# Split products of a two-block decoder: the moving columns and their results walked from the last column to the first

## The reference, cut to what matters

```python
q = (hf @ w_query).reshape(T, PEER_HEADS, 2, D_KEY // 2)
s1 = jnp.einsum("thk,hnk->thn", q[:, :, 0], sub_keys1)
s2 = jnp.einsum("thk,hnk->thn", q[:, :, 1], sub_keys2)
...                                       # top 16 of 16384 experts for each token and head
u = expert_down[ib]                       # (128 tokens, 8 heads, 16, 1024)
act = jax.nn.gelu(jnp.einsum("td,thkd->thk", hb, u), approximate=False)
v = expert_up[ib]
return jnp.einsum("thk,thkd->td", gb * act, v)
```

## Time and profile before

| | |
|---|---|
| time, median of 3 runs | 2018.89 us (2018.7 to 2019.29) |
| profiled execution: span from first to last instruction | 2015.2 us |
| PE busy | 1988.4 us, 99% of the span |
| DVE, ACT busy | 1512.0 us (75%), 1025.4 us (51%) |
| TensorE clock granted, mean | 0.996 |
| DMA | 219 GB/s in the mean |

### The profile page before, as it was taken

One profiled execution on the slowest core, in us unless ns is written; L12 is line 12 of the kernel. 1 busy time (PEld: TensorE's weight loads), 2 busy tenths in 40 slices (PEclk: granted clock), 3 DMA queues, 4 the chain that ended last, 5 costly groups with the idle time before them and its releaser, 6 DMA issues.

```text
span 2015.2 us, 38041 instructions
## 1 busy us (share of the span) xinstructions
PE 1988.4 (99%) x14231; PEld 1842.9 (91%) x14231; DVE 1512.0 (75%) x2628; ACT 1025.4 (51%) x1394; POOL 0.2 (0%) x4
## 2 busy tenths in 40 slices
PE   9999999999999999999999999999999999999998
PEld 8888999999999888888899999999999998888886
DVE  6777779988885666666679665888888866666666
ACT  6741454455555444444546553544555554444444
POOL 0000000000000000000000000000000000000000
PEclk8999999999999999999999999999999999999999
DMA  8555767776566777777655655777766677777776
GB/s 302 177 200 190 280 202 243 237 246 200 186 187 217 238 243 238 243 240 242 208 170 168 189 165 179 226 237 229 235 196 186 187 226 238 244 238 242 239 245 189
DMA packets 136462, 440.85 MB, mean 219 GB/s; under 512 B 15136, under 2 KB 15392, under 8 KB 133920
## 3 DMA queue, kind: packets, MB, share of 16 engines
q1 hardware_dynamic: 118496, 406.84, 64.5%
q10 hardware_dynamic: 17856, 32.51, 4.4%
HBM read 403.64 MB, written 35.65 MB: 218 GB/s over the span
## 4 chain that ended last, share of the span: by engine, by line
PE 91%; DVE 5%; DMA 2%; ACT 1%; issue 1%; SPq 0%; DVEq 0%; ACTq 0%
PE ps L581 27%; PE ps L582 27%; PE ps L583 27%; PE ps L913 3%; DVE ring_lo L394 2%; PE ps L618 1%; DMA ring<-in_wq 1%; PE ps L631 1%; PE ps L761 1%; PE ps L889 1%; ACT ring_hi L388 1%; DMA arena<-in_w_ada 0%; DMA ring<-in_down 0%; DVE arena L1979 0%; DVE arena L1544 0%
## 5 line engine op out<-in xcount | busy, mean ns | idle before, releaser
L394 DVE TENSOR_TENSOR ring_lo<-ring,ring_hi 128x1024 fp32r<-128x1024 f32 x632 | 772.6, 1223 | 289.1 <-ACT ring_hi L388 285.3
L388 ACT ACTIVATE ring_hi<-ring 128x1024 fp32r<-128x1024 f32 x632 | 667.9, 1057 | 601.4 <-PE ps L583 496.1
L581 PE MATMUL ps<-h_hi,ring_lo 128*128 128x256 f32 x2816 | 801.6, 285 | 11.0 <-DVE ring_lo L394 8.6
L582 PE MATMUL ps<-h_lo,ring_hi 128*128 128x256 f32 x2816 | 789.0, 280 | 0.0
L583 PE MATMUL ps<-h_hi,ring_hi 128*128 128x256 f32 x2816 | 788.9, 280 | 0.0
L581 PEld LDWEIGHTS ps<-h_hi,ring_lo 128*128 128x128 f32 x2816 | 535.5, 190 | 15.0 <-issue 7.7
L582 PEld LDWEIGHTS ps<-h_lo,ring_hi 128*128 128x128 f32 x2816 | 532.8, 189 | 0.4 <-issue 0.2
L583 PEld LDWEIGHTS ps<-h_hi,ring_hi 128*128 128x128 f32 x2816 | 530.6, 188 | 0.0
L583 PE MATMUL ps<-ring_hi,w_hi 128*128 128x512 f32 x1024 | 399.0, 390 | 0.0
L581 PE MATMUL ps<-ring_hi,w_lo 128*128 128x512 f32 x1024 | 399.0, 390 | 0.0
L582 PE MATMUL ps<-ring_lo,w_hi 128*128 128x512 f32 x1024 | 399.0, 390 | 0.0
(11 more groups left out here) (300 smaller groups left out, 1331.4 us busy)
## 6 DMA issues: line engine op xcount, KB each, us to landing
ring<-in_down SPq DMA_DIRECT2D x256, 512.0 KB, 4.3
ring<-in_up SPq DMA_DIRECT2D x256, 512.0 KB, 4.0
ring<-in_w_in SPq DMA_DIRECT2D x72, 512.0 KB, 3.6
kept_z<-wf ACTq DMA_DIRECT2D x124, 256.0 KB, 3.2
xT<-kept_z SPq DMA_DIRECT2D x124, 256.0 KB, 4.2
arena<-in_w_ada SPq DMA_DIRECT2D x16, 1024.0 KB, 8.9
ring<-in_wq SPq DMA_DIRECT2D x32, 512.0 KB, 4.2
arena<-in_w_ada SPq DMA_DIRECT2D x16, 512.0 KB, 8.2
```

The costliest lines, as they stand in the source:

```text
L388: nc.scalar.activation(ring_hi[:, part_slot(m), :], ring[:, slot(m), :], ACT.Copy).then_inc(S("high"), 1)
L394: ns.tensor_tensor(ring_lo[:, part_slot(n), :], ring[:, slot(n), :], ring_hi[:, part_slot(n), :].bitcast(fp32), ALU.subtract)\
L581: mm(psum, s_lo, m_hi, start=start, stop=False)
L582: mm(psum, s_hi, m_lo, start=False, stop=False)
```

## The change

`product` turns three views round along their last axis before it issues its three matmuls: the PSUM destination and both parts of the moving operand.

```diff
             def product(psum, stat, move, start, stop):
 
                 (s_hi, s_lo), (m_hi, m_lo) = stat, move
+                psum, m_hi, m_lo = psum[:, ::-1], m_hi[:, ::-1], m_lo[:, ::-1]
                 mm(psum, s_lo, m_hi, start=start, stop=False)
                 mm(psum, s_hi, m_lo, start=False, stop=False)
                 return mm(psum, s_hi, m_hi, start=False, stop=stop)
```

## The result

The changed kernel takes **2045.64 us** (median of 4 runs, 2044.11 to 2046.88). The kernel before took 2018.80 us in the median of four runs (2006.13 to 2019.29); the ratio is 1.0165, with a 95% interval of 1.0135 to 1.0195. So the change costs between 1.4 and 2.0%, about 27 us. Before's own runs scatter: one of the four lies 13 us under the other three, and 13 more, taken later with the experiments, have a median of 2009.52 us. All runs of the changed kernel lie above all of them.

What follows compares the result with a forecast made beforehand. The prediction took PE's product matmuls, times the distance between their starts, to bound the kernel. A span of 2015.2 us, plus 0 for the change and 3.7 us around it, gave 2018.9 us; the range was 1987 to 2090 us.

Steps and rivals of the forecast that it cites:

- Rival B: Every product matmul: walking backwards, each crossing between memory stretches costs twice, 68 us more, about 2087 us; chance 0.06.
- Rival D: 256-column products: the 113.1 and 117.8 ns regimes shift; 1987 to 1996 us (chance 0.09) or 2029 to 2039 us (0.06).
- What bounds the kernel: On PE: 12,096 product matmuls times the distance between their starts, about 1.74 ms; DVE, ACT and DMAs lie beside it.
- The place: Product matmuls at full clock: a surcharge along the columns, 6.5 and 13.6 ns, on which a turned direction acts.
- Read of the moving columns: Product matmuls' moving operand, step -1 for +1: same elements and neighbours, so 0 us.
- Write of the sums: Product matmuls' PSUM write, step -1: all three matmuls of a product are turned alike, so 0 us.
- Rival A: Every product matmul: a backwards walk gets one column per half-clock cycle, 1484 us more, about 3503 us; chance 0.15.
- Rival C: Product matmuls: the surcharge vanishes, together 53 us faster, about 1966 us; chance 0.05.
- The weight load: 256-column matmuls: the unturned weight load bounds them at 108 ns, hiding the change if only 512-column steps move.

## Why the prediction was right and wrong

The time lies in the range, near its middle, but the forecast, 2018.9 us and no change, did not happen. By the sign that the prediction set itself, a distance that moves by more than a third of a nanosecond, it was wrong: by 4.7 ns at 300 us and by 6.5 ns at 700 us. That the range holds the time is partly luck. It was drawn around rivals B and D, and what came is D's places together with half of B's price on 512 columns, a case that the list does not have.

- *What bounds the kernel*: right. The loss is product matmuls times the distance of their starts, 27 of 29.9 us by the sum above; nothing beside PE moved. One check in it was loose: 1.74 ms is 86% of the span, and the chain's share of the three lines is 81%.
- *The place*: right. "at full clock something along the columns (the read of the moving operand, or the write of the sums) is just not keeping pace" is where the loss came from, and the half-clock stretch, still at 213 ns, bears it out. The runs settle which of the two it is: the read.
- *Read of the moving columns, "I take 0"*: **the step that failed.** It measured 6.5 ns on 512 columns, 20 us in all, and the loss of the faster regime on 256 columns, 10 us. The argument was that both walks touch the same elements, each next to the one before. Inside 64 bytes the order indeed made no difference; the order of the stretches inside 256 bytes did: the argument looked at too small a scale. The same goes for the rule of the Trainium skill, page "SBUF — State Buffer", section "SBUF: two separate sides": a walk backwards hits each line of 16 bytes four times, and the read-only run still took 1.0181 of before.
- *Write of the sums, 0*: right, 226.9 ns and 1.0018 (0.9995 to 1.0041). The rule of the Trainium skill, page "Advanced Engine Details and Errata", section "Memory Cachelines", would slow matmuls with any pattern that is not contiguous; here a step of -1 on the write cost nothing, and neither did swapped pairs on read and write.
- *Rival A* (half pace): did not happen. *Rival B*: right that the order of stretches of memory counts, wrong in its mechanism and size. Not every crossing downwards costs: stretches of 256 bytes and more walked downwards kept 226.8 ns, and a walk upwards that skips stretches (even, then odd) cost more than the reversal, 240.0 ns. B doubled the surcharge, 13.6 ns more; measured were 6.5 ns, half as much again. *Rival C*: no walk tried had less surcharge than the forwards one.
- *Rival D*: its place was right (256 columns at 117.8 in all stretches, 10 us), the cause that it gave, a small change in when columns are read, is not shown: the counts above say that the backwards read takes the faster regime away, not how. And the reason against it does not hold: three runs within 0.6 us were taken to say that "the program fixes" the regime, but before's runs reach from 2002.09 to 2019.29 us. The 0.2% that the prediction took for the limit of what can be told from no change falls with it: one program spreads over 0.9%.
- *The weight load* as what would hide a change on 256 columns, and as C's bound: not borne out. With loads of 0.14 in place of 0.19 us the 256-column matmuls stood no closer, 119.1 and 118.4 ns.

## What to carry to other kernels

On a TensorE-bound kernel with float32r operands, read the moving columns so that each 256 bytes of a partition come upwards in address and without a gap. Swapping neighbours, walking such 256-byte stretches in descending order, and the direction of the PSUM write were free here; the stretches were tried with 512 columns alone. Before arguing that a change of order is free because "the same elements are neighbours", look in the trace for a pace that is already short of one column per cycle: 226.8 instead of 213.2 ns said that something along the columns was at its limit, and here the order of larger stretches counted. Compare a stream's pace with that of the same instruction at half clock: a surcharge that is there at full clock alone marks the place on which a change of order can act. And take more than three runs before you call a spread of 0.6 us the noise.

## What the runs showed of the hardware that was not expected

- The surcharge of a 512-column float32r matmul over 213.2 ns is 13.6, 20.1 or 26.8 ns by the order of its 64-byte stretches (about 1, 1.5 or 2 cycles at 2.4 GHz for each), and walks with positive steps alone can be the worst (240.0 ns, read and write permuted alike).
- 256-column matmuls have two paces forwards, 113.1 and 117.8 ns, which last for hundreds of microseconds and lie in other stretches from one profiled kernel to the next, though these read 256 columns alike; read backwards, all are at 117.8. They are worth some 10 us of this kernel. What chooses between them stays open.
- Loading 64 stationary columns in place of 128 shortened the load from 0.19 to 0.14 us and did not make a matmul cheaper: 230.0 against 226.8 ns forwards, 233.3 in both cases backwards.
